# Loading two expert keys per DMA, and routing at 11/8 keys a part, in a one-core decoder layer

## The reference

```python
def peer_ffn(xn, w_q, sub_keys, u, v):
    q = (t @ w_q).reshape(T, PEER_HEADS, 2, PEER_HALF)
    s = jnp.einsum('thpd,hpnd->thpn', q, sub_keys)
    s_top, i_top = lax.top_k(s, PEER_TOPK)                 # top 16 of 128, twice per head
    cand_s = s_top[:, :, 0, :, None] + s_top[:, :, 1, None, :]
    best_s, pos = lax.top_k(cand_s, PEER_TOPK)             # top 16 of the 256 pairs
    ids = take_along_axis(cand_i, pos)                     # 8 heads x 16 experts of 16384
    gates = softmax(best_s)
    act = gelu(einsum('td,ted->te', x_c, u[ids_c]))
    return einsum('te,ted->td', gates * act, v[ids_c])
```

## Time and profile before

| | us |
|---|---|
| three runs of the kernel | 1035.52, 1036.67, 1038.79 |
| median | 1036.67 |
| the profiled execution (it is the slowest of these) | 1038.79 |
| its span, from first to last instruction | 1037.0 |
| TensorE busy | 1013.3 |
| VectorE busy | 746.6 |
| u keys on TensorE, first to last | 296 to 681 |
| v keys on TensorE, first to last | 681 to 1031 |

### The profile page before, as it was taken

One profiled execution on the slowest core, in us unless ns is written; L12 is line 12 of the kernel. 1 busy time (PEld: TensorE's weight loads), 2 busy tenths in 40 slices (PEclk: granted clock), 3 DMA queues, 4 the chain that ended last, 5 costly groups with the idle time before them and its releaser, 6 DMA issues.

```text
span 1037.0 us, 19662 instructions
## 1 busy us (share of the span) xinstructions
PE 1013.3 (98%) x6891; PEld 938.7 (91%) x6891; DVE 746.6 (72%) x1438; ACT 561.4 (54%) x951; POOL 447.3 (43%) x280
## 2 busy tenths in 40 slices
PE   6999999999999999999999999999999999999997
PEld 6998899898999999999999999978888888888886
DVE  5766565535999999999864677756677777677774
ACT  6785555544455454444454766745555454545453
POOL 1000001010188888888888888222333332233331
PEclk9999999999999999999999999999999999999999
DMA  9589655424257777777777776658676777777772
GB/s 308 191 305 337 223 201 201 155 82 147 98 99 187 180 194 181 191 187 184 182 188 185 162 159 162 174 183 258 228 236 225 227 226 234 228 229 223 238 227 82
DMA packets 122207, 204.99 MB, mean 198 GB/s; under 512 B 34864, under 2 KB 81968, under 8 KB 122032
## 3 DMA queue, kind: packets, MB, share of 16 engines
q1 hardware_dynamic: 94512, 204.27, 61.3%
q0 software_dynamic: 27648, 0.11, 6.5%
HBM read 190.62 MB, written 13.73 MB: 197 GB/s over the span
## 4 chain that ended last, share of the span: by engine, by line
PE 88%; DVE 7%; ACT 2%; DMA 1%; issue 1%; SPq 0%; POOL 0%; DVEq 0%; ACTq 0%; POOLq 0%
PE acc L1385 33%; PE acc L1165 17%; PE bank L1337 11%; PE bank L1338 11%; PE bank L1339 11%; DVE wsp L747 2%; PE bank L1360 1%; DMA wblk<-wmap 1%; DVE hl L968 1%; DMA wraw<-w_in 1%; ACT wsp L411 1%; PE bank L1269 1%; PE bank L1247 1%; PE bank L1194 0%; DVE topi L983 0%
## 5 line engine op out<-in xcount | busy, mean ns | idle before, releaser
L386 POOL DMA_INDIRECT wmap<-gate,widx x192 | 319.3, 1663 | 102.9 <-issue 58.2
L1385 PE MATMUL acc<-hl,whl 128*128 128x512 f32 x1152 | 266.8, 389 | 1.6 <-DVE whl L1082 1.6
L651 ACT ACTIVATE hl<-raw 128x1024 fp32r<-128x1024 f32 x192 | 202.9, 1057 | 120.4 <-PE acc L1385 111.5
L1385 PEld LDWEIGHTS acc<-hl,whl 128*128 128x128 f32 x1152 | 216.1, 188 | 47.2 <-issue 1.8
L968 DVE TENSOR_TENSOR hl<-raw,hl 128x1024 fp32r<-128x1024 f32 x153 | 187.2, 1229 | 66.2 <-ACT hl L651 64.2
L1337 PE MATMUL bank<-xt,hl 128*128 128x256 f32 x768 | 219.2, 285 | 0.2 <-DVE hl L968 0.2
L392 POOL TENSOR_TENSOR act_w<-act_w,wblk 128x384 f32 (+1 forms) x64 | 110.0, 1719 | 251.4 <-DMA wblk<-wmap 233.5
L1339 PE MATMUL bank<-xt,hl 128*128 128x256 f32 x768 | 217.3, 283 | 0.0
L1338 PE MATMUL bank<-xt,hl 128*128 128x256 f32 x768 | 217.3, 283 | 0.0
L1337 PEld LDWEIGHTS bank<-xt,hl 128*128 128x128 f32 x768 | 147.3, 192 | 0.7 <-issue 0.7
L1338 PEld LDWEIGHTS bank<-xt,hl 128*128 128x128 f32 x768 | 147.4, 192 | 0.2 <-issue 0.2
(11 more groups left out here) (217 smaller groups left out, 1332.0 us busy)
## 6 DMA issues: line engine op xcount, KB each, us to landing
raw<-u_t SPq DMA_DIRECT2D x128, 512.0 KB
raw<-v SPq DMA_DIRECT2D x128, 512.0 KB
wmap<-zeros SPq DMA_DIRECT2D x6, 2048.0 KB, 11.4
wblk<-wmap SPq DMA_DIRECT2D x64, 192.0 KB, 3.5
wraw<-w_in SPq DMA_DIRECT2D x9, 1024.0 KB, 8.4
wraw<-w_pq SPq DMA_DIRECT2D x8, 1024.0 KB, 5.2
wraw<-w_ck SPq DMA_DIRECT2D x4, 1024.0 KB, 7.6
wraw<-w_cv SPq DMA_DIRECT2D x4, 1024.0 KB, 8.2
```

The lines of the kernel that those rows point to most:

```text
L386: nc.gpsimd.indirect_dma_start(out=wmap, out_offset=bass.IndirectOffsetOnAxis(ap=set_ranks(widx, k)[:, h, r:r + 1], axis=0), in_=set_ranks ...
L651: nc.scalar.activation(eslot(k, 0, second), raw[:, k // 2, k % 2], ACT.Copy).then_inc(ready, 1)
L1385: last = pe.matmul(acc[:, 2 * t + n], a, b[:, 512 * n:512 * n + 512], start=False, stop=last_key and k == 2, skip_group_check=True)
```

## The change

Two edits. First, the raw loads: SP loads a pair of keys with one DMA of 1 MB in place of two of 512 KB. There are two semaphores `s_raw` in place of four, SP waits for the split of the second key of the pair before in place of each key's own, and ScalarE waits for a landing only at the even keys. Second, `part_key`: the routing parts follow each other at 11/8 of a key in place of 3/2, so the last one falls into iteration 68 in place of 74; the batches' `gate_exp` and `gates` move with them (batch 4's `gates` from iteration 78 to 72, batch 3's from 30 to 28, batch 2's stays at 12).

```diff
-        s_raw = [sem(f"s_raw{i}") for i in range(4)]
+        s_raw = [sem(f"s_raw{i}") for i in range(2)]
...
         def part_key(n):
-            return -(-3 * (n - PARTS0 + 1) // 2) - 1
+            return -(-11 * (n - PARTS0 + 1) // 8) - 1
...
-            for k in range(4):
-                sp.dma_start(raw[:, k // 2, k % 2], u_t[k // 2][:, k % 2]).then_inc(s_raw[k], 16)
+            for q in range(2):
+                sp.dma_start(raw[:, q], u_t[q]).then_inc(s_raw[q], 16)
             with sp.Fori(1, KEYS // 4) as it:
-                for k in range(4):
-                    sp.wait_ge(s_ul, it * 4 - 4 + (k + 1))
-                    sp.dma_start(raw[:, k // 2, k % 2],
-                                 u_t[ds(it * 2 + k // 2, 1)].rearrange("o p j d -> (o p) j d")[:, k % 2]).then_inc(s_raw[k], 16)
-            for k in range(4):
-                sp.wait_ge(s_ul, KEYS - 4 + k + 1)
-                sp.dma_start(raw[:, k // 2, k % 2], vd[k // 2][:, k % 2]).then_inc(s_raw[k], 16)
+                for q in range(2):
+                    sp.wait_ge(s_ul, it * 4 - 4 + 2 * q + 2)
+                    sp.dma_start(raw[:, q], u_t[ds(it * 2 + q, 1)].rearrange("o p j d -> (o p) j d")).then_inc(s_raw[q], 16)
+            for q in range(2):
+                sp.wait_ge(s_ul, KEYS - 4 + 2 * q + 2)
+                sp.dma_start(raw[:, q], vd[q]).then_inc(s_raw[q], 16)
...
             with sp.Fori(1, KEYS // 4) as it:
                 for q in range(2):
-                    for k in (2 * q, 2 * q + 1):
-                        sp.wait_ge(s_vl, it * 4 - 4 + (k + 1))
-                        sp.dma_start(raw[:, q, k % 2],
-                                     vd[ds(it * 2 + q, 1)].rearrange("o i j d -> (o i) j d")[:, k % 2]).then_inc(s_raw[k], 16)
+                    sp.wait_ge(s_vl, it * 4 - 4 + 2 * q + 2)
+                    sp.dma_start(raw[:, q], vd[ds(it * 2 + q, 1)].rearrange("o i j d -> (o i) j d")).then_inc(s_raw[q], 16)
                     sp.wait_ge(s_A, it * 2 + q - 1)
                     sp.dma_start(wblk[:, q], wm[:, ds(it * (2 * WBK) + WBK * q, WBK)]).then_inc(s_wb[q], 16)
...
             def split_high(k, landed, free, ready, second=False):
                 if landed is not None:
-                    act.wait_ge(s_raw[k], landed)
+                    act.wait_ge(s_raw[k // 2], landed)
...
-                landed = 16 * ((j + 4) // 4 + 1)
+                n = (j + 4) // 2
                 if j < KEYS - 4:
-                    split_high(j % 4, landed, (s_um, j + 1), s_uh)
+                    split_high(j % 4, 16 * (n // 2 + 1) if j % 2 == 0 else None, (s_um, j + 1), s_uh)
```

More of the change, by code:

```diff
@@ L682, in _ @@
                 if u > U_PQ + 5:
-                    split_high(u - U_PQ - 6, 16, None, s_uh)
+                    split_high(u - U_PQ - 6, 16 if u == U_PQ + 6 else None, None, s_uh)
             key_rows(PH - 1)
             for k in (2, 3):
-                split_high(k, 16, (s_seed, 1) if k == 2 else None, s_uh)
+                split_high(k, 16 if k == 2 else None, (s_seed, 1) if k == 2 else None, s_uh)
             gate_exp(1)
@@ L695, in _ @@
                 gelu(j)
-                landed = 16 * ((j + 4) // 4 + 1)
+                n = (j + 4) // 2
                 if j < KEYS - 4:
-                    split_high(j % 4, landed, (s_um, j + 1), s_uh)
+                    split_high(j % 4, 16 * (n // 2 + 1) if j % 2 == 0 else None, (s_um, j + 1), s_uh)
                 elif j < KEYS - 1:
-                    split_high(j % 4, landed, (s_um, j + 1), s_vh, second=True)
+                    split_high(j % 4, 16 * (n // 2 + 1) if j % 2 == 0 else None, (s_um, j + 1), s_vh, second=True)
                 if exps < len(BATCHES) and j == batch_key(exps) + 2:
@@ L715, in _ @@
                         a_high(k, k)
-            split_high(3, 16 * (KEYS // 4 + 1), (s_um, KEYS), s_vh, second=True)
+            split_high(3, None, (s_um, KEYS), s_vh, second=True)
             act.wait_ge(s_fx, KEYS - ROUTE0)
@@ L720, in _ @@
                 for k in range(4):
-                    split_high(k, (it + 2) * 16 + 16 * (KEYS // 4), (s_vm, it * 4 + (k + 1)), s_vh, second=True)
+                    split_high(k, (it + 2) * 16 + 16 * (KEYS // 4) if k % 2 == 0 else None, (s_vm, it * 4 + (k + 1)), s_vh, second=True)
                     if k % WBK == 0:
```

## The result

The changed kernel takes 1045.16 us (median of four runs, 1044.32 to 1045.64), the kernel before, run beside it, 1037.48 (four runs, 1035.52 to 1038.79). The ratio is 1.0080, with a 95% interval of 1.0061 to 1.0098. It is slower, and by more than such runs scatter: all nine executions of it on record lie between 1043.98 and 1048.24, the profiled one at 1045.10.

The account below looks back on a forecast made before the run. TensorE bounds, with VectorE level beside it during the routing. At key 77, 0.1 (routing) + 3.4 (light windows) + 1.1 (`gate_exp`) + 4.5 (empty window) make 9.1 us; on the median 1036.67 this gives 1046, range 1040 to 1057.

Parts of the forecast that it names:

- ledger of VectorE's prices: Routing stretch: sum of VectorE's splits, parts and `gates` up to a key; put key 40 3.6 us late, key 77 0.1.
- pair's later issue, its whole landing: u stage: an even key's load waits for split j-3, not j-4, and lands whole; VectorE idles L - 0.9 - parts.
- L: Time from issue to landing of a 1 MB raw load in the routing stretch, taken as 5.4 us.
- Light windows: Waits for a pair covered by only two light routing parts: 0.7 us each at keys 10, 32, 38, 54, 60; 3.4.
- `gate_exp` at key 15: ScalarE's `gate_exp` with two table loads of 1.28 makes keys 15 and 16 late: 1.1 us.
- The empty window: After the last routing part (iteration 68) VectorE has no parts to cover the landing: 4.5 us at keys 75 and 76.
- The larger counts: Of the delays at key 40 (6.7 us) and key 77 (9.1 us) the kernel pays only the larger, 9.1.
- What would show it: Signs after: `hl` waits of TensorE 8 to 10 us, frequent ScalarE waits, last part near 514, v keys 2.72.
- The v stage and the turn: Pair loads in the v stage and at the turn from u to v cost 0 each.
- Rival B: v stage: `wblk` becomes a bound as well, 10.6 to 10.9 against 10.88 us; some 8 us more, 1054; chance 0.11.
- A: Only the denser routing shows, as pairs land in under 4.7 us: 3.6 to 4.4, 1040.3 to 1041; chance 0.13.
- C: No change, TensorE stays the only bound and key 40's 3.6 us are gone: 1036.7, at best 1034.9; chance 0.14.

Follow-up runs that it names:

- late_halves: `routing_alone` with SP waiting in the u stage as for a pair but then sending two 512 KB loads: 1041.69 us, ratio 1.0035.
- gates_4_later: The changed kernel with `gates` 4 four iterations later, in iteration 76: 1043.52 us, ratio 1.0055 to the kernel before.
- gates_in_two: The changed kernel with the eight copies of `gates` 3 two iterations later: 1046.61 us, ratio 1.0077 to the kernel before.
- both_gates: The changed kernel with the edits of `gates_in_two` and `gates_4_later` together: 1043.78 us, ratio 1.0064 to the kernel before.
- routing_alone: The kernel before with the routing at 11/8 keys a part, its 512 KB loads left as they are: 1041.14 us, ratio 1.0038.
- routing_5_4: The kernel before with the routing at 5/4 keys a part and single loads: 1050.90 us, ratio 1.0141.
- stall_b: The kernel before with the low part computed again, five times more for key 37 and eight for key 88: 1046.03 us (one run).

## Why the prediction was right, and where it was not

**The bound.** TensorE with VectorE level beside it while the routing runs: right. The ledger of VectorE's prices held to 0.6 wherever it was tried: 3.6 against 4.0 us for the routing alone at key 40 (all of it lost by key 33), 1.8 against 2.4 at key 18, and 13.3 against 13.6 at 5/4 keys a part. The worth of `gates` 4 being earlier was 0 as said. The last scatter even starts later, at 661.2 in place of 655.2, since the 192 scatters took 1697 ns each in place of 1663; SP sends the first `wblk` at 676.83, so nobody felt it.

**The pair's later issue, its whole landing.** The mechanism was right and the size of one term off. From issue to ScalarE's copy an even key of the changed kernel takes 4.74 to 5.49, with a median of 4.9 (34 pairs, keys 8 to 74), not 5.4. The 6.1 that bounded L from above was not typical of a half load either: in `late_halves` they take 3.8 to 4.8 from issue to copy. VectorE's idle times in the changed kernel, timeline, 316 to 526, are these five, and 0.15 at key 10:

```profile
338.27 1.23 DVE L965 TENSOR_TENSOR hl3u<-raw,hl3u 128x1024 fp32r<-128x1024 f32 x1 [0.28 <-ACT hl3u L648]
...
388.91 1.23 DVE L965 TENSOR_TENSOR hl<-raw,hl 128x1024 fp32r<-128x1024 f32 x1 [0.39 <-ACT hl L648]
...
454.92 1.25 DVE L965 TENSOR_TENSOR hl<-raw,hl 128x1024 fp32r<-128x1024 f32 x1 [0.58 <-ACT hl L648]
...
514.48 1.23 DVE L965 TENSOR_TENSOR hl3u<-raw,hl3u 128x1024 fp32r<-128x1024 f32 x1 [1.42 <-ACT hl3u L648]
518.54 1.29 DVE L972 TENSOR_TENSOR hl<-raw,hl 128x512 fp32r<-128x512 f32 x2 [2.83 <-ACT hl L648]
```

Light windows: 0.15, 0.39 and 0.58 at three keys (10, 32 and 54), 1.1 in place of the 3.4 predicted at five. `gate_exp` at key 15: 0.28 in place of 1.1. The empty window: 1.42 and 2.83 at keys 75 and 76, 4.25 against 4.5. Together 5.65 against 9.0. The prediction had worked out 5.6 for a landing of 4.9, and key 77 comes 5.9 later (6.4 from key 0). The step that was off is the choice of L = 5.4: the 16.5% that the scatters take of the DMA engines did not lengthen the landing beyond the 4.9 of the lone load.

The Trainium skill ("DMA: Bandwidth & Descriptors", Anatomy of one DMA) fits 2.0 us plus bytes over 436 GB/s, an estimate of 4.4 for 1 MB. The page has this fit for DMAs that GpSimd issues, and these are issued by SP. In the trace of after no copy of an even key started under 4.74 after the issue, so for this sum the measurement decides for about 4.9. Each pair's last DMA packet ends 4.4 to 5.1 after the issue there, 4.5 in the median, near the estimate; ScalarE's start comes some 0.4 later.

**"The larger counts".** Right as a rule. The prediction took key 77, with 9.1 there against 6.7 at key 40. In the first trace key 77 is indeed the last that is late, by 0.32, with 6.4 against 6.0; in the second nothing is late behind key 35, and both are at 6.0. A step was missing from the path to key 40: the 1.57 us that TensorE loses to its own clock behind the wait at key 33. In short:

| | predicted | found |
|---|---|---|
| routing alone, key 40 | 3.6 | 4.0 |
| light windows, `gate_exp` up to key 40 | 3.1 | 0.8 (gates_4_later, 4.8 at key 40, less the 4.0) |
| the clock behind key 33 | none | 1.57, there in both traces of the changed kernel, not in gates_4_later |
| key 40 | 6.7 | 6.0 |
| key 77 | 9.1 | 6.4 and 6.0 |

The 1045.2 measured against the 1046 predicted flatters the working: 2.7 us too much at key 77, set against a median of before that came out 0.8 higher than the one I had, and 1.3 of scatter. That a total so near came out is in part luck.

**What would show it.** TensorE's `hl` waits: 4.6 us in the waits view and 6.7 by late keys with the clock's share, not 8 to 10; at 17, 18, 33 and 77 as said, not at 40 and 62. ScalarE's many waits: 40. The last routing part ended at 510.8, three us earlier than the 514 that I gave it, and 9.5 earlier than before; v keys stayed at 2.72.

**The v stage and the turn.** 0 and 0 were right. Windows of the kernel after, to be set beside the second row:

```profile
706.00:1021.00 315.00, 315.00 (x1391) 260.82 (x1390) 184.77 (x234) 161.31 (x234) 62.68 (x59) 1.00 0.65 231
```

The same 1391 matmuls in 315 us. Rival B had no margin by my sum, 10.6 to 10.9 of 10.88, because it took 1.97 for the weigh from the earlier trace rows. The weigh takes 1.02 once it starts later, which gives the margin back. The price of B was mis-added too: 0.3 to 0.5 in each of 30 rounds is 9 to 15 us, not 8. And the 3.53 that it reads as the wait for `wblk` is GpSimd's idle time. What shows `wblk` behind the raw loads is its own landing, the last number here, before and after:

```profile
wblk<-wmap SPq DMA_DIRECT2D x64, 192.0 KB, 3.5
...
wblk<-wmap SPq DMA_DIRECT2D x64, 192.0 KB, 4.7
```

**Which rivals fell.** A (only the denser routing shows) was the nearest: the routing is 4.0 of 6.4. It fell because a pair takes 4.9 to ScalarE's copy and not under 4.7. C fell: nothing made key 40's lateness go away. As for a better version, none of the kernels tried beat the one before, and none of these edits can win more than the 1.8 us that TensorE waits there.

**Left open.** How the 1.3 (or 0.9) us over the sum of the parts divide: in the traces it is the clock's fall and the path to key 77, of about equal size. Either alone is enough: `gates_in_two` has no fall and is at 6.7. Two traces have neither, `gates_4_later` and `both_gates`, at 4.9 and 5.3. Whether each further run of the changed kernel had the fall, its total does not say. Why the scatters take 1697 ns in place of 1663 is open as well. The denser routing alone does not explain it: they take 1704 in `routing_alone`, but 1684 in the still denser `routing_5_4`, and 1689 in `stall_b`, whose routing is that of before.

## What to carry to other kernels

A batched transfer is issued later and must land whole before its first part is used. Price both as landing minus the work that the consumer still has, window by window: the dear window is the one in which that work has just run out. Whether the later issue costs anything depends on the slack behind that window; in `late_halves` it cost 2.3 us of VectorE and nothing of the kernel, while in the changed kernel the same 2.3 lie on a path to key 77 that was as long as the one that bounds. Where a second engine is level with the bound, keep a ledger of its prices up to each deadline; it was good to 0.6 us here, and the delay is the largest over the deadlines, not their sum. An engine that waits 83 us for a DMA may cost nothing (ScalarE in `late_halves`), while a wait of 1.9 us on the engine that bounds costs 3.5.

## What the runs showed of the hardware that was not expected

**TensorE's granted clock fell behind its longer waits.** Behind keys late by 1.89, 2.04 and 3.13 us it went to 0.50 about 0.4 to 1.5 us after TensorE had resumed, for some 3.4 us, and cost 1.57 more; behind one late by 4.36 it was at 0.50 from the first matmul, for some 5 us, and cost 2.34. Keys late by up to 1.87 showed nothing of it.

**The weigh and a_low hold each other up.** In the v stage before, GpSimd's weigh takes 1.74 us in the mean and VectorE's a_low 0.77; after, 1.06 and 0.42. In the trace of before a weigh (798.72 to 800.58) and an a_low (799.63 to 800.87, 1.24 long) overlap; 50 of the 117 a_lows between 700 and 1015 are as long. In the trace of after one is, and the a_low has passed when the weigh comes:

```profile
800.50 0.42 DVE L1079 TENSOR_TENSOR whl<-act_w,whl 128x256 fp32r<-128x256 f32 x1
...
800.86 1.02 POOL L389 TENSOR_TENSOR act_w<-act_w,wblk 128x384 f32 x1 [4.50 <-DMA wblk<-wmap]
```

Where they met it looks like a queue of one: a split ran from 798.49 to 799.72, the weigh that had begun beside it ended 0.86 after that, and the a_low begun beside the weigh ended 0.29 after the weigh. The Trainium skill ("SBUF — State Buffer", SBUF: two separate sides) says that VectorE's instructions with two SBUF inputs and GpSimd's share a port pair that is locked for a whole instruction, so that the other blocks. The traces agree: 1.24 against 0.42 for the same instruction. They do not show a blocking to the last tenth: after the other had ended the weigh ran 0.86 more where it takes 1.02 alone, and the a_low 0.29 where it takes 0.42. It cost the kernel nothing, as TensorE was the bound.
